# Start addresses of the fp32r tiles that the weight streams read

## The reference

```python
def reference(x, ...):
    x = first_block(x, ...)     # h = rms_norm(x); h @ w_in (2048 x 7536); sparse attention and RWKV-7 mixers
                                # x += mixed @ w_out (2048 x 2048); x += hier_moe(rms_norm(x))
    return second_block(x, ...) # mod = silu(c) @ w_ada (2048 x 12288); h @ w_in, h @ w_gate; three mixers
                                # x += g1 * norm(merged @ w_o); x += g2 * norm(relu(h @ w_up)**2 @ w_down)

def hier_moe(h, ...):           # 4 groups of 4 experts, each 2048 -> 512 -> 2048
    ...
    for e in range(N_EXPERTS):
        he = jax.nn.silu(t @ w_e_gate[e]) * (t @ w_e_up[e])
        y = y + combine[:, e:e + 1] * (he @ w_e_down[e]).astype(f32)
    return y.reshape(B, S, D).astype(h.dtype)
```

## Time and profile before

| | us |
|---|---|
| median of 3 runs | 3223.1 |
| span of the profiled execution | 3220.3 |
| PE busy | 3075.7 (96%) |
| DVE busy | 2066.5 (64%) |
| ACT busy | 1513.0 (47%) |

### The profile page before, as it was taken

How to read it: one execution, slowest core, us unless ns; L and a number is a source line. 1 busy time by engine, 2 the same in 40 slices (tenths; PEclk the granted TensorE clock), 3 DMA queues, 4 the chain that set the end, 5 groups by cost and what they waited for, 6 DMA issues and landing times. The chain is left out here.

```text
span 3220.3 us, 43840 instructions
## 1 busy us (share of the span) xinstructions
PE 3075.7 (96%) x17864; PEld 2446.1 (76%) x17864; DVE 2066.5 (64%) x2332; ACT 1513.0 (47%) x1822; POOL 20.1 (1%) x10
## 2 busy tenths in 40 slices
PE   8999978998899999999999989999997999999997
PEld 7888855966787776666688878877776888888885
DVE  5557547365868787785558868755666556555555
ACT  4345432143656566563444475555444444444443
POOL 0000001000000000000000000000000000000000
PEclk9999978999999999999999999999999999999998
DMA  7979868087978788793576654575766555555551
GB/s 265 337 262 341 288 212 338 4 303 293 342 270 321 264 295 306 254 345 131 160 234 209 225 180 148 191 245 167 267 209 231 174 183 184 190 186 183 187 189 68
DMA packets 358321, 739.09 MB, mean 230 GB/s; under 512 B 19977, under 2 KB 118422, under 8 KB 344583
## 3 DMA queue, kind: packets, MB, share of 16 engines
q1 hardware_dynamic: 342916, 711.64, 64.3%
q10 hardware_dynamic: 15236, 25.06, 2.1%
HBM read 710.00 MB, written 26.65 MB: 229 GB/s over the span
## 5 line engine op out<-in xcount | busy, mean ns | idle before, releaser
L286 DVE TENSOR_TENSOR moe_w_lo<-ring,moe_w_hi 128x1024 fp32r<-128x1024 f32 x384 | 461.5, 1221 | 163.7 <-ACT moe_w_hi L276 156.2
L276 ACT CAST moe_w_hi<-ring 128x1024 fp32r<-128x1024 f32 x384 | 402.3, 1049 | 277.6 <-PE psum L302 274.5
L286 DVE TENSOR_TENSOR mx_w_lo<-ring,mx_w_hi 128x1024 fp32r<-128x1024 f32 (+1 forms) x288 | 347.1, 1210 | 281.8 <-ACT mx_w_hi L276 277.8
L286 DVE TENSOR_TENSOR mlp_w_lo<-ring,mlp_w_hi 128x1024 fp32r<-128x1024 f32 x256 | 313.5, 1225 | 293.3 <-ACT mlp_w_hi L276 292.2
L276 ACT CAST mx_w_hi<-ring 128x1024 fp32r<-128x1024 f32 (+1 forms) x288 | 297.1, 1038 | 424.2 <-PE psum L302 409.2
L276 ACT CAST mlp_w_hi<-ring 128x1024 fp32r<-128x1024 f32 x256 | 268.4, 1049 | 418.0 <-PE psum L302 418.0
L302 PE MATMUL psum<-mx_w_hi,mx_a_hi 128*128 128x496 f32 (+1 forms) x1024 | 405.8, 396 | 6.8 <-DVE mx_w_lo L286 4.9
L302 PE MATMUL psum<-mx_w_lo,mx_a_hi 128*128 128x496 f32 (+1 forms) x1024 | 398.1, 389 | 0.0
L302 PE MATMUL psum<-mx_w_hi,mx_a_lo 128*128 128x496 f32 (+1 forms) x1024 | 397.9, 389 | 0.0
L286 DVE TENSOR_TENSOR in_w_lo<-ring,in_w_hi 128x628 fp32r<-128x628 f32 x192 | 155.3, 813 | 185.5 <-ACT in_w_hi L276 184.3
L302 PE MATMUL psum<-in_w_hi,in_a_hi 128*128 128x314 f32 x768 | 244.1, 318 | 1.7 <-DVE in_w_lo L286 1.2
(11 more groups left out here) (604 smaller groups left out, 5582.8 us busy)
## 6 DMA issues: line engine op xcount, KB each, us to landing
ring<-in_w_ada SPq DMA_DIRECT2D x72, 1024.0 KB, 9.1
ring<-in_w_e_gate SPq DMA_DIRECT2D x64, 1024.0 KB, 5.5
ring<-in_w_e_up SPq DMA_DIRECT2D x64, 1024.0 KB, 6.3
ring<-in_w_e_down SPq DMA_DIRECT2D x64, 1024.0 KB, 5.2
ring<-in_w_up SPq DMA_DIRECT2D x64, 1024.0 KB, 5.2
ring<-in_w_down SPq DMA_DIRECT2D x64, 1024.0 KB, 5.1
ring<-in_w_in SPq DMA_DIRECT2D x64, 992.0 KB, 5.1
ring<-in_w_in SPq DMA_DIRECT2D x96, 628.0 KB, 5.5
```

The costliest lines, as they stand in the source:

```text
L276: self.nc.scalar.copy(self.w[0][:, self._half(j, half), :, 0:cols], self.view[:, slot, ks, 0:cols]).then_inc(self.hi_done, 1)
L286: self.nc.vector.tensor_tensor(self.w[1][:, q, :, 0:cols], self.view[:, j % self.slots, ks, 0:cols], self.w[0][:, q, :, 0:cols].bitcast(F3 ...
```

## The change

No instruction is added, removed or moved; on all engines they stand in the same order as before. What changes are start addresses in SBUF. A parameter asks the allocator for a multiple of `align` bytes: 512 for the `w` and `a` tiles of `Split`, `heT` of the mlp and `m` of the mixers, and 64 for the tiles of the experts. The small routing tiles are allocated ahead of the large ones, and a row of `rt.slot_parts` becomes PITCH = 280 elements (1120 bytes) long, of which 278 are used.

```diff
-    def __init__(self, stage, ring, act, body, ready=None, slots=RING, width=NB, view=None):
+    def __init__(self, stage, ring, act, body, ready=None, slots=RING, width=NB, view=None, align=512):
...
-        self.w = [stage.sb(f"w_{n}", [P, 4, self.HALF, width], F32R) for n in ("hi", "lo")]
-        self.a = ready if self.ready else [stage.sb(f"a_{n}", [P, KT, S], F32R) for n in ("hi", "lo")]
+        self.w = [stage.sb(f"w_{n}", [P, 4, self.HALF, width], F32R, align) for n in ("hi", "lo")]
+        self.a = ready if self.ready else [stage.sb(f"a_{n}", [P, KT, S], F32R, align) for n in ("hi", "lo")]
...
-    def sb(self, name, shape, dt=F32):
-        return self.ctx.enter_context(self.chip.nc.sbuf_tensor(f"{self.name}_{name}", shape, dt))
+    def sb(self, name, shape, dt=F32, align=32):
+        return self.ctx.enter_context(self.chip.nc.sbuf_tensor(f"{self.name}_{name}", shape, dt, align_bytes=align))
...
+PITCH, ALIGN = 280, 64
...
-        sb = lambda n, s, dt=F32: ctx.enter_context(nc.sbuf_tensor(f"rt_{n}", s, dt))
-        self.parts = [sb(f"a_{n}", [P, KT, S], F32R) for n in ("hi", "lo")]
-        self.slot_parts = [sb(f"s_{n}", [P, KT, SLOTS], F32R) for n in ("hi", "lo")]
+        sb = lambda n, s, dt=F32, align=32: ctx.enter_context(nc.sbuf_tensor(f"rt_{n}", s, dt, align_bytes=align))
         self.order = sb("order", [P, NG], mybir.dt.int32)
         self.share, self.slot_share = sb("share", [P, T, EPG]), sb("slot_share", [P, NG, EPG])
+        self.parts = [sb(f"a_{n}", [P, KT, S], F32R, ALIGN) for n in ("hi", "lo")]
+        self.slot_parts = [sb(f"s_{n}", [P, KT, PITCH], F32R) for n in ("hi", "lo")]
...
-        split = Split(st, ring, None, body, ready=rt.parts)
-        heT = [st.sb(f"heT_{n}", [P, KC, S], F32R) for n in ("hi", "lo")]
+        split = Split(st, ring, None, body, ready=rt.parts, align=ALIGN)
+        heT = [st.sb(f"heT_{n}", [P, KC, S], F32R, ALIGN) for n in ("hi", "lo")]
...
-        heT = [st.sb(f"heT_{n}", [P, KC, S], F32R) for n in ("hi", "lo")]
+        heT = [st.sb(f"heT_{n}", [P, KC, S], F32R, 512) for n in ("hi", "lo")]
...
-        self.parts = [st.sb(f"m_{n}", [P, KT, S], F32R) for n in ("hi", "lo")]
+        self.parts = [st.sb(f"m_{n}", [P, KT, S], F32R, 512) for n in ("hi", "lo")]
```

More of the change, by code:

```diff
@@ L1481, in _ @@
                     sc.wait_ge(gathered, k + 1)
-                    nc.scalar.activation(rt.slot_parts[0][:, k], gather(k), ACT.Identity,
+                    nc.scalar.activation(rt.slot_parts[0][:, k, 0:SLOTS], gather(k), ACT.Identity,
                                          scale=gain[:, k:k + 1]).then_inc(hi_made, 1)
@@ L1571, in _ @@
                     ve.wait_ge(hi_made, k + 1)
-                    nc.vector.scalar_tensor_tensor(rt.slot_parts[1][:, k], gather(k), gain[:, k:k + 1],
-                                                   rt.slot_parts[0][:, k].bitcast(F32), ALU.mult,
+                    nc.vector.scalar_tensor_tensor(rt.slot_parts[1][:, k, 0:SLOTS], gather(k), gain[:, k:k + 1],
+                                                   rt.slot_parts[0][:, k, 0:SLOTS].bitcast(F32), ALU.mult,
                                                    ALU.subtract).then_inc(lo_made, 1)
```

## The result

The changed kernel takes 3204.78 us (median of 4 runs, 3202.4 to 3208.09), the kernel before 3223.2. The ratio is 0.9943, interval 0.9931 to 0.9956, which is 14 to 22 us. When it ran once more beside some of the experiments it took 3204.48 us, ratio 0.9931, interval 0.9915 to 0.9948. The forecast was 3207.1 in a range of 3198 to 3216: faster, by 16 us; it is 18.4. The profiled execution took 3206.84 us, in the upper half of the four.

What follows compares the result with a forecast made beforehand. PE's pace through the 9792 matmuls of line 302 after `in` sets the end; 9.4 + 2.3 + 4.3 = 16.0 us off the 3220.3 span gives 3204.3, plus 2.8 from span to median 3207.1, range 3198 to 3216.

Steps and rivals of the forecast that it cites:

- (a): mlp_heT, offsets 128/352 to 0/0: 1536 matmuls go from 233.3 to 227.2 ns, 9.4 us off.
- (d): mx_a, mlp_a, wout and moe_heT: offsets equal before and after, so 0.
- (b): mx_m, offsets 128/352 to 0/0: 384 matmuls go from 233.3 to 227.2 ns, 2.3 us off.
- (c): rt_a, offsets 480/96 to 256/256: 768 matmuls go from 232.4 to 226.8 ns, 4.3 us off.
- rivals 3 and 4: Starts at a multiple of 512 are bad (rival 3), or better still, another 96 us off, 3111 (chance 0.05).
- rival 3: Starts at a multiple of 512 are bad: mx_a, mlp_a and wout lose 6.1 ns a matmul, 3249.3 us; chance 0.04.
- (e): rt_s, 1152 matmuls with mixed offsets before and after: taken as 0, bounds 6.0 us less to 1.7 us more.
- (f): in, 2304 matmuls of 314 columns, already at the surplus of equal offsets: 0, with 2.3 us kept on both sides.

Runs made afterwards that it cites:

- the first sweep: The changed kernel with stationary tiles moved against w at 0: wout_a to 32, mx_a to 64, mx_m to 96, mlp_a to 128, mlp_heT to 160; 3237.4 us.

## Why the prediction was right

**What bounds the kernel.** Held for the streams that changed: in the experts, mx_m and the mlp the gain in pace came out at the end. That "PE never waits there" is a little too strong, since PE is idle for 9 of the 734 us of the earlier trace rows in the mlp. And it does not hold of all 9792 matmuls: in `mx_a` at 224 some 7 us came out of 9.4 or more.

**(a) mlp_heT, 9.4 us.** 1536 x (233.3 - 226.7) = 10.1 by the pace. The forecast was slightly undersized, because the fast pace was taken from mlp_a at 227.2. mlp_a gained too, which (d) had at 0: by windows that open at the second start it went at 226.9 and 227.1 in turn before and at 226.7 to 226.8 after, some 0.4 us for its 1536. The stretch of both became 10.7 us shorter in the first profile and 9.5 in three others with the same mlp addresses (743.9 to 744.0).

**(b) mx_m, 2.3 us.** 384 x 6.6 = 2.5 by the pace, 2.2 by the stretch.

**(c) rt_a, 4.3 us.** 768 x (232.4 - 226.8) = 4.3 by the pace of the round in the earlier trace rows; two of the four rounds were at 233.4 before, which makes it 4.7.

**(d) the other streams with equal offsets, 0.** Held: 0/0 is as good as 128, 320 and 480, and rivals 3 and 4 fell with it. The size of rival 3, 6.1 ns a matmul, was real: a kernel with wout_a, mx_a, mx_m, mlp_a and mlp_heT at a bad difference ran 30 us over the changed one.

**(e) rt_s, 0.** 384 x 0.5 more, 384 x 1.2 and 384 x 1.6 less, and moe_heT with 86 tokens, also put at 0, 3.4 ns less in three of its four rounds (144 matmuls): 1.4 us less in all, within the bounds. The change of moe_heT is the one that the prediction had excluded, since its tiles were at equal offsets before and after. Beside (c) this fits the 5.7 us of the experts' stretch without the routing; with the routing it is 5.0.

**(f) in, 0.** Held, -0.4 us.

**The number.** The forecast of 16.0 us lies within the measured 14 to 22. The stretches of the changed streams became 18.6 us shorter (10.7, 2.2 and 5.7), and the medians differ by 18.4; that these two agree so closely is in part luck, since the profiled span is only 15.3 us shorter, with 1.2 us lost ahead of the routing, 0.7 in it and 1.7 in `mx_a`.

**The step that was wrong** without harm to the number is the rule itself: "whether the row of `w` that streams and the piece of `a` that is loaded meanwhile begin at the same offset within 512 bytes". The modulus is 256, and the pair is not enough; hi and lo must agree as well. All differences of the kernel before (224 and 128) were bad modulo 256 too, and no two of its full streams differed by 256, so its trace could not tell; that the change put every tile of a stream at one offset, where both rules agree, is what kept the number whole. It cost a whole expectation: the sweep with two tiles at 256 was forecast at 3246 to 3250 and ran in 3214.9. The rule of the Trainium skill (SBUF — State Buffer, section Who interferes with whom) has PE read its moving operand and its weights through independent ports and wait on no one. The table of differences does not agree with that: addresses alone move the pace of the same instructions between 226.7 and 234.3 ns.

## What to carry to other kernels

Where matmuls with full stationary pieces and 512 columns of fp32r follow each other and PE sets the end, give the moving and the stationary tiles, hi and lo, one offset modulo 256 bytes; here this was worth 6.6 ns in 233 for each, some 3%, and needs no instruction. The rows of w here are 2048 bytes apart; no run shows other row lengths of full width. Measure it as the distance between starts in an unbroken run, stream by stream, since the whole time scatters by as much as one stream's gain. Before padding for it, look whether the stream has anything above the surplus of the good ones: the 314-column stream had not.

## What the runs showed beyond that

With rows of 496 columns the same addresses have more than one pace, and a run of matmuls keeps the one that it begins with. In the first sweep (difference 64) one run of 190 matmuls went at 41.58 / 189 = 220.0 ns and the next, 8 us later and 766 matmuls long, at 173.40 / 765 = 226.7. With all tiles at 224 it was 220.0 for one run and 224.4 for another:

```profile
1623.23:1664.81 41.58, 41.58 (x190) 35.49 (x189) 1.00 0.75 246
1672.17:1843.87 171.70, 171.70 (x766) 144.07 (x765) 1.00 0.65 210
```

With equal offsets it is 223.3 in every run. So 220.0 is possible, 3.3 ns better than what the kernel has, but no address found holds it. By an estimate of one column for each cycle of 2.4 GHz 496 columns take 206.7 ns and 512 take 213.3; the surplus of 496 columns is then 13.3 ns at the best pace and 20.0 at the worst, the same sizes as those of the good pace and of the commonest bad one with 512 (13.4 and 20.0). Other cases of two paces at the same addresses are mlp_a at 16 and mlp_heT at 240 bytes, rt_a of the kernel before (233.4 and 232.4), and its moe_heT with 86 tokens (233.3 in three rounds, 230.0 in one). What makes a run take one pace or the other no run here shows. Nor is it known what the 13.4 ns over the estimate for 512 columns are, which no address took away.
